# A two-block transformer layer on one core: order of bank copies in a step, chains spread over steps, a first load in six pieces, and w_o in 256 columns

## What is computed

```python
def first_block(x, mem, norm_mix, w_in, ...):
    mem_n = rmsnorm(mem, mem_norm)
    h = x
    for i in range(DEPTH):                                   # DEPTH = 1
        h = h + hybrid_mixer(rmsnorm(h, norm_mix[i]), w_in[i], ...)
        h = h + memory_cross_attention(rmsnorm(h, norm_xa[i]), mem_n, w_q[i], w_k[i], w_v[i], w_o[i])
        h = h + swiglu(rmsnorm(h, norm_ffn[i]), w_gate[i], w_up[i], w_down[i])
    return rmsnorm(h, norm_final)

def hybrid_mixer(h, w_in, ...):
    proj = h @ w_in
    z, xbc, dt_raw, sc_u, sc_b, sc_c = jnp.split(proj, IN_SPLITS, axis=-1)
...
    y_ssd = grouped_rmsnorm(y * jax.nn.silu(z), ssd_norm, SSD_GROUPS)
    v = sc_b * causal_dwconv(sc_c * sc_u, sc_conv_w)
    y_sc = grouped_rmsnorm(v, sc_norm, SC_GROUPS)
    return jnp.concatenate([y_ssd, y_sc], axis=-1) @ w_out

def second_block(x, ...):
...
        h = rmsnorm_2(x, norm_mix[i])
        p = h @ w_in[i]
        x = x + jnp.concatenate([y_a, y_b, y_c], axis=-1) @ w_out[i]   # pool, hyena and gated mixers of p
        h = rmsnorm_2(x, norm_ffn[i])
        up = dwconv3(h @ ffn_w_up[i], ffn_conv_w[i], ffn_conv_b[i])
        gate, val = jnp.split(up, 2, axis=-1)
        x = x + (jax.nn.silu(gate) * val) @ ffn_w_down[i]
    return rmsnorm_2(x, norm_final)
```

## Time and profile before

| | us |
|---|---|
| median of three executions | 2703.28 (2701.18 to 2703.99) |
| the profiled execution | 2696.7 |
| its span | 2694.9 |
| PE busy | 2639.1 |
| DVE busy | 1923.0 |
| ACT busy | 1498.2 |
| POOL busy | 391.0 |

### The profile page before, as it was taken

One profiled execution on the slowest core, in us unless ns is written; L12 is line 12 of the kernel. 1 busy time (PEld: TensorE's weight loads), 2 busy tenths in 40 slices (PEclk: granted clock), 3 DMA queues, 4 the chain that ended last, 5 costly groups with the idle time before them and its releaser, 6 DMA issues.

```text
span 2694.9 us, 38678 instructions
## 1 busy us (share of the span) xinstructions
PE 2639.1 (98%) x15034; PEld 2275.4 (84%) x15034; DVE 1923.0 (71%) x2919; ACT 1498.2 (56%) x2315; POOL 391.0 (15%) x390
## 2 busy tenths in 40 slices
PE   8999999999999999999999999999999999999998
PEld 7888888887788788888888878888888888888887
DVE  7777767868877665656565689687877677776775
ACT  6555658686555444444444456545555555555554
POOL 2111002225301010010101034011201010101012
PEclk9999999999999999999999999999999999999999
DMA  6555565565555555666666656536666666666664
GB/s 229 180 182 186 178 197 178 175 208 184 164 172 174 173 160 166 189 190 188 193 188 189 191 166 210 168 120 182 186 189 193 189 190 190 191 189 189 192 180 127
DMA packets 136559, 490.78 MB, mean 182 GB/s; under 512 B 15415, under 2 KB 16248, under 8 KB 136376
## 3 DMA queue, kind: packets, MB, share of 16 engines
q1 hardware_dynamic: 135656, 486.21, 59.6%
q10 hardware_dynamic: 720, 2.10, 0.2%
HBM read 486.12 MB, written 2.13 MB: 181 GB/s over the span
## 4 chain that ended last, share of the span: by engine, by line
PE 87%; DVE 8%; ACT 2%; issue 2%; DMA 0%; SPq 0%; DVEq 0%; ACTq 0%
PE ps L792 55%; PE ps L789 28%; DVE wl L1322 2%; ACT wh L1028 1%; DVE hT L1322 1%; DVE X L1328 1%; DVE A L1328 1%; PE ps L964 0%; PE ps L997 0%; DVE T L1328 0%; PE ps L806 0%; DVE T L1322 0%; DVE R L1322 0%; DVE Gf L1322 0%; DMA raw<-in_w_sc 0%
## 5 line engine op out<-in xcount | busy, mean ns | idle before, releaser
L1322 DVE TENSOR_TENSOR wl<-raw,wh 128x1024 fp32r<-128x1024 f32 (+1 forms) x905 | 1140.0, 1264 | 709.1 <-ACT wh L1028 708.6
L792 PE MATMUL ps<-X,wh 128*128 128x512 f32 x4848 | 1628.4, 397 | 11.9 <-DVE T L1322 5.4
L1028 ACT ACTIVATE wh<-raw 128x1024 fp32r<-128x1024 f32 (+1 forms) x905 | 953.2, 1056 | 951.6 <-PE ps L789 920.1
L789 PE MATMUL ps<-X,wl 128*128 128x256 f32 x4848 | 1225.5, 278 | 0.0
L792 PEld LDWEIGHTS ps<-X,wh 128*128 128x128 f32 x4848 | 892.6, 188 | 214.4 <-issue 10.3
L789 PEld LDWEIGHTS ps<-X,wl 128*128 128x128 f32 x4848 | 878.6, 188 | 24.0
L792 PE MATMUL ps<-XG,wh 128*128 128x512 f32 x2240 | 761.3, 399 | 21.8 <-DVE hT L1322 21.1
L789 PE MATMUL ps<-XG,wl 128*128 128x256 f32 x2240 | 571.1, 280 | 0.0
L792 PEld LDWEIGHTS ps<-XG,wh 128*128 128x128 f32 x2240 | 413.7, 189 | 118.0 <-DVE hT L1322 27.4
L789 PEld LDWEIGHTS ps<-XG,wl 128*128 128x128 f32 x2240 | 409.4, 189 | 11.4
L1792 POOL TENSOR_TENSOR hT<-hT,T 128x256 f32<-128x256 f32 x224 | 188.6, 863 | 1442.2 <-DVE hT L1322 1442.2
(11 more groups left out here) (192 smaller groups left out, 1172.0 us busy)
## 6 DMA issues: line engine op xcount, KB each, us to landing
raw<-in_w_gate SPq DMA_DIRECT2D x176, 512.0 KB, 3.8
raw<-in_w_down SPq DMA_DIRECT2D x176, 512.0 KB, 3.7
raw<-in_w_sc SPq DMA_DIRECT2D x95, 512.0 KB, 4.2
raw<-in_w_up SPq DMA_DIRECT2D x88, 512.0 KB, 3.7
raw<-in_w_val SPq DMA_DIRECT2D x88, 512.0 KB, 4.0
raw<-in_w_zx SPq DMA_DIRECT2D x80, 512.0 KB, 4.0
raw<-in_w_in SPq DMA_DIRECT2D x68, 512.0 KB, 3.7
raw<-in_w_osc SPq DMA_DIRECT2D x32, 512.0 KB, 3.7
```

What stands on the lines that cost most here:

```text
L789: t = e.matmul(bank(c, i)[:, 0:256], wl[:, b0:b0 + 128], X[:, kx * 512:kx * 512 + 256], start=False, stop=sp and kk == c.kn - 1)
L792: e.matmul(bank(c, i)[:, :], wh[:, b0:b0 + 128], X[:, kx * 512:kx * 512 + 512], start=st and kk == 0, stop=False)
L1028: return e.activation(out, in_, ACT.Copy, scale=scale)
L1322: return e.tensor_tensor(out, a, b, op)
```

## The change

It has five parts. (1) In each step the pieces `ev`, `res`, `resn` and `vcopy` are sorted to the front, ahead of the split. (2) Chains between ACT and DVE are cut into pieces of different steps: norms get `nfinb` one step behind `nfin` (with `nmm` a step later), `nfin2` gets `nfin2b`, `sn1` gets `sn1b`, `sn2` gets `sn2h` (ACT) and `sn2l` (DVE), `mgain` `mgainl`, `prod` `prodh`/`prodl`; dt5 and dt6, `zim`, `zi` and the memory's `mgain` from the fifth on move to later steps; the `evs` of the first `hv` column and of `gate` wait for the norm. (3) x comes in six loads (1, 1, 2, 4, 4, 4 tiles), of which SP issues the last three between the loads of units. (4) `w_o` uses 24 matmuls of 256 columns a unit, all into the left half, and its `resn` has two adds. (5) After steps with pieces of the scan a new matmul order, `TWOS`, is used.

```diff
         if c.kind == "rn":
-            rd += 4
+            rd += 2 if c.src == "w_o" else 4
...
-    for k, step in enumerate((0, 0, 1, 1, 2, 3, 4, 4, 5, 6, 7, 7)):
+    for k, step in enumerate((0, 0, 1, 1, 3, 3, 4, 4, 5, 6, 6, 7)):
         put(step, "xgain", 4 + k)
...
     for p in range(8):
-        put((s + 3, s + 4, s + 7, s + 8, s + 9, s + 10, s + 11, s + 12)[p], "mgain", 2 * p)
-        put(s + 3 + p + (p > 1), "nsq", (1, p))
-    put(s + 12, "nmm", 1)
-    put(s + 13, "nfin", 1)
+        d = (22, 24, 27, 28, 29, 30, 32, 33)[p]
+        put(s + d, "mgain", 2 * p)
+        put(s + d + 1, "mgainl", 2 * p)
+        put(s + 22 + p, "nsq", (1, p))
+    put(s + 31, "nmm", 1)
+    put(s + 32, "nfin", 1)
+    put(s + 33, "nfinb", 1)
...
             put(e + 1, "ev", c)
-            put(e + 1, "evs", c)
+            put(max(e + 1, U_O + 5) if c.kind == "gate" else max(e + 1, U_DOWN[0][-1].last + 6) if c.kind == "hv" else e + 1, "evs", c)
...
-                put(e + 2 + n + (n > 4), "dt%d" % n, c)
-            put(e + 8, "acsw", 0)
+                put(e + 2 + n + 3 * (n > 4), "dt%d" % n, c)
+            put(e + 9, "acsw", 0)
...
-                put(b + 9, "sn1", g)
-                s = max(b + 11, U_OSC[g // 2] + 1)
+                put(b + 10, "sn1", g)
+                put(b + 11, "sn1b", g)
+                s = max(b + 12, U_OSC[g // 2] + 1)
                 for n in range(2):
                     put(s + n, "sn2", (g, n))
+                    put(s + n + 1, "sn2h", (g, n))
+                    put(s + n + 2, "sn2l", (g, n))
...
-                    put(e + 2, "nmm2", 0)
+                    put(e + 3, "nmm2", 0)
                 if ni < 6:
-                    put(e + 2, "nmm", ni)
-                    put(e + 3, "nfin", ni)
+                    put(e + 3, "nmm", ni)
+                    put(e + 4, "nfin", ni)
+                    put(e + 5, "nfinb", ni)
...
-                    put(e + 4, "nfin2", 0)
+                    put(e + 5, "nfin2", 0)
+                    put(e + 6, "nfin2b", 0)
                     for k in range(16):
-                        put(e + 6 + k // 2, "hscale", k)
+                        put(e + 7 + k // 2, "hscale", k)
...
-                    put(b + 7 + i, "zim", 3 * hf + i)
-                    put(b + 8 + i, "zi", 3 * hf + i)
-                b += 11
+                    put(b + 8 + i, "zim", 3 * hf + i)
+                    put(b + 9 + i, "zi", 3 * hf + i)
+                b += 12
...
+    for step in at:
+        at[step].sort(key=lambda p: p[0] not in ("ev", "res", "resn", "vcopy"))
     return at
...
+TWOS = [(k, i, m) for k in range(4) for m in range(2) for i in range(2)]
+STATE = {"cbm", "ssd0", "ssd3", "sn0"}
...
-XCH = ((0, 2), (2, 4), (4, 8), (8, 12), (12, 16))
+XCH = ((0, 1), (1, 2), (2, 4), (4, 8), (8, 12), (12, 16))
...
-        for u in range(1, NRAW):
-            load(u)
-        e.dma_start(par[:, 16:NPAR], T_["par"][:, 16:NPAR]).then_inc(d_par, 16)
...
+        load(1)
+        loadx(3)
+        load(2)
+        load(3)
         for s in STEPS:
             for piece, i in PLAN[s]:
                 if piece == "split" and i + NRAW < NU:
                     load(i + NRAW)
+                    if i in (1, 2):
+                        loadx(3 + i)
...
+            elif c.src == "w_o":
...
+                    for i in range(2):
+                        b0 = (u % NW) * UN + kk * 256 + 128 * i
+                        e.matmul(bank(c, i)[:, 0:256], wh[:, b0:b0 + 128], xh, start=kk == 0, stop=False)
+                        e.matmul(bank(c, i)[:, 0:256], wh[:, b0:b0 + 128], xl, start=False, stop=False)
+                        t = e.matmul(bank(c, i)[:, 0:256], wl[:, b0:b0 + 128], xh, start=False, stop=kk == 3)
```

More of the change, by code:

```diff
@@ L230, in schedule @@
         put(step, "split", step + 3)
-    for k, step in enumerate((0, 0, 1, 1, 2, 3, 4, 4, 5, 6, 7, 7)):
+    for k, step in enumerate((0, 0, 1, 1, 3, 3, 4, 4, 5, 6, 6, 7)):
         put(step, "xgain", 4 + k)
-    for p in range(8):
[L234 to L241, removed]
-        put((s + 3, s + 4, s + 7, s + 8, s + 9, s + 10, s + 11, s + 12)[p], "mgain", 2 * p)
-        put(s + 3 + p + (p > 1), "nsq", (1, p))
-    put(s + 12, "nmm", 1)
-    put(s + 13, "nfin", 1)
-    put(s + 15, "memT", 0)
-    put(s + 16, "memc", 0)
+    for p, step in enumerate((2, 2, 3, 4, 5, 5, 6, 7)):
+        put(step, "nsq", (0, p))
+    put(8, "nmm", 0)
+    put(9, "nfin", 0)
+    put(10, "nfinb", 0)
+    s = of("z")[-1].last
+    for j in range(4):
+        put(s + 18 + 2 * j, "mload", j)
+    for p in range(8):
+        d = (22, 24, 27, 28, 29, 30, 32, 33)[p]
[5 more added lines that the diff above has]
+    put(s + 33, "nfinb", 1)
+    put(s + 35, "memT", 0)
+    put(s + 36, "memc", 0)
     for c in COLS:
@@ L346, in schedule @@
             put(e + 3, "prod", c)
+            put(e + 4, "prodh", c)
+            put(e + 5, "prodl", c)
         if c.kind == "gate" and c.i == 0:
@@ L400, in schedule @@
                 for n in range(3):
[L401 removed]
+                    put(c.first + (4, 7, 9)[n], "hout", n)
             for i in range(2):
@@ L428, in unit_orders @@
     for a, b in zip(starts, starts[1:] + [NU]):
-        order += [SIX if q == 0 else HEAD if q % 4 == 0 else EVEN for q in range(b - a)]
+        if any(piece in STATE for piece, i in PLAN.get(a - 1, ())):
+            order += [TWOS if q == 0 else HEAD if q % 4 == 1 else EVEN for q in range(b - a)]
+        else:
+            order += [SIX if q == 0 else HEAD if q % 4 == 0 else EVEN for q in range(b - a)]
     order[0] = EVEN
@@ L477, in program @@
     d_mem = [sem(f"d_mem{i}") for i in range(4)]
-    d_x = [sem(f"d_x{i}") for i in range(5)]
+    d_x = [sem(f"d_x{i}") for i in range(6)]
     d_w0 = [sem(f"d_w0_{i}") for i in range(4)]
@@ L1230, in scalar @@
                     e.activation(sacc(i), vT, ACT.Sqrt).then_inc(snA, 1)
-                if piece == "sn2":
+                if piece == "sn2h":
                     g, n = i
@@ L1255, in scalar @@
                         e.activation(Sb(i, n), Sb(i, n), ACT.Silu).then_inc(gs, 1)
-                if piece == "prod":
+                if piece == "prodh":
                     for n in range(2):
@@ L1340, in vector @@
                        ALU.subtract).then_inc(lo, 1)
-                if piece == "mgain":
+                if piece == "mgainl":
                     for k in (i, i + 1):
@@ L1363, in vector @@
                 if piece == "nfin":
-                    ps, y, u = banks[4 if i in (2, 4, 5) else 6][:, 0:256], rsb(i), tile(10 if i == 1 else 8)
+                    ps = banks[4 if i in (2, 4, 5) else 6][:, 0:256]
                     w.wait_ge(nmm, i + 1)
@@ L1476, in vector @@
                     w.wait_ge(mm, c.last + 1)
-                    for m in range(2):
+                    for m in range(1 if c.src == "w_o" else 2):
                         for n in range(2):
@@ L1574, in vector @@
                     w.wait_ge(snv, 5 * i)
-                    ts(v, banks[6][:, 0:256], 1.0 / 512, 1e-5, ALU.mult, ALU.add).then_inc(snv, 1)
+                    ts(vT, banks[6][:, 0:256], 1.0 / 512, 1e-5, ALU.mult, ALU.add).then_inc(snv, 1)
+                if piece == "sn1b":
+                    v, u, y = vT, sacc(i), srs(i)
                     w.wait_ge(snA, i + 1)
@@ L1625, in vector @@
                         tt(Sb(c, n), Sb(c, n), Sb(gate, n), ALU.mult).then_inc(pr, 1)
+                if piece == "prodl":
+                    c = i
                     for n in range(2):
```

30 lines of the change are left out of this document (22 added, 8 removed).

## The result

| | before | after |
|---|---|---|
| median, us | 2702.23 (4 runs) | 2659.56 (4 runs, 2658.39 to 2660.43) |
| profiled execution / its span | 2696.7 / 2694.9 | 2659.41 / 2657.6 |
| TensorE idle in the span | 55.8 | 27.1 |

The ratio is 0.9843, 95% interval 0.9826 to 0.9860: 42.7 us faster by the medians, 37.3 us by the two profiled executions. The forecast was 36.8 us and 2666.5 us. The kernels of the experiments ran later, beside the kernel before at medians of 2698.30, 2700.59 and 2700.21 us, so their medians are compared with 2659.56 only roughly, and what a part is worth is read from the profiles.

The account below looks back on a forecast made before the run. TensorE's work plus 55.8 us of standing still was taken as the bound, with gains only where VectorE is full. Ten terms summed to 36.8 us, so 2703.3 - 36.8 = 2666.5 us, range 2656 to 2684.

Parts of the forecast that it names:

- (a): Rival: nearly every wait goes, also at the memory norm, and the border costs nothing; gain 50 us, 2653 us; chance 0.12.
- (c): Rival, ordinary columns: sorted adds wait for TensorE's last matmul and hold up the split; slower, 2711 us; chance 0.02.
- (d): Rival: start and norms gain, but half of the banks' waits stay; time within 0.2% (5.4 us); chance 0.02.
- Rival (b): The split becomes late at the memory norm, the output projections and after zim; gain 19 us, 2684 us; chance 0.14.
- Start: First four units: the last quarter loads sooner and the half clock ends sooner; +4.3 us (3 to 5.5).
- Scan: Stretch 440 to 656 us: three waits go with the cut sn2 and the sort; +3.6 us.
- at nothing: The TWOS order, prodh/prodl and the extra issues on SP: counted as no gain, +-1 us in all.
- Memory norm: 650 to 702 us: five hT waits, about 14 us; VectorE bounds, earlier free banks help; +5 us (2.5 to 9).
- w_o: At w_o, a 2.87 us wait goes, 4.7 with extras, less 0.9 for 24 matmuls; +3.9 us (0 to 4).
- Output projections: 1500 to 1626 us: waits worth 7.7 us go as banks come free first; +7.0 us (4 to 8).
- Border: 1626 to 1680 us: old waits go, +3.1, but new waits of 3.6 and 2.0 come; -2.5 us (-5 to +2).
- zim: At zim: 3.52 us idle and a short wait, 5.5 with refill and clock; +4.9 us (2 to 6).

Follow-up runs that it names:

- the experiments on mgain, the transposes and the squares: Changed kernel with later mgain pairs: 2660.68 us; three table edits plus memT, memc three steps later: 2655.67 us; squares' sums cut to 16 columns: 2653.89 us.

## Why the prediction was right, and where not

**The frame held, and the sum was lucky.** A sum over places by TensorE's stalls gave 36.8 us for 37.3 measured between the profiles; no term has the wrong sign. But the terms miss by 0.1 to 3.1 us each, 13 us without regard to sign, and the misses cancel: the forecast is 6.7 us too low in four terms and 6.2 too high in the other six. The bounds given for the terms add up to 19.2 and 49.0 us, not to the 22 and 46 that the prediction names. Rivals (a), (c) and (d) fell. Rival (b), the split that comes late, is real at one place only, the one that the forecast had already charged.

**The basis was off by 6.6 us.** I subtracted the gain from the median, 2703.3, and got 2666.5; 2696.7 less 36.8, the profiled execution, would have been 2659.9 for 2659.56 measured. The changed kernel's profile is at its own median, the one of before was under its own. Part is the start: of four profiles with the old loads the one of before has the earliest unit 12, 1.4 us under their mean. The granted clock is another part: 37 executions of the kernel before in the later comparisons, its repeat included, run from 2694.7 to 2703.5 us, and the thirteen at a mean clock of 0.995 have a mean time of 2698.3 us, the thirteen at 0.993 one of 2700.1, the four at 0.991 or 0.992 one of 2702.6. The clocks of the three executions whose median I took are not recorded, so how the 6.6 us divide stays open.

**Start, +4.3, measured +2.1.** The load part of the mechanism is right: in all ten profiles with the new loads the first unit ends earlier (10.7 to 12.9 us) than in the four with the old ones (13.3 to 14.0). In size it is 3.1 us at unit 3 and 2.9 at unit 12 by the means of all profiles, at the lower bound of 3; the queues moved 422 GB/s in 9:11 after 416, so the rate is not what was missing. The clock part is not shown. It stands at 1.00 in 9:11 instead of 0.50, but it does so in the other three profiles with the old loads too, and in five of the ten with the new loads it is at 0.50. And +2.1 is counted from a profile of before with an early unit 12, 52.6 us; in its repeat, where the clock fell at the first norm, it is 54.3. I named the table's new steps of the squares as room and did not walk the first norm through with them. Its matmul stalls 1.45 us where it didn't before, and its second wait is 1.3 shorter. One table entry takes most of the second wait away (+1.5 at unit 12).

**Scan, +3.6, measured +6.7.** The three waits went as priced: without the new order the place still gains 3.7. The other 3.0 us are the step "at nothing", the TWOS order with the cover that a unit's length doesn't depend on it. It does: 2.77 was the length in the plain stretch, and I took it for the whole kernel. Before, 51 of the 160 units from 40 to 199 take 2.82 or 2.83 us; after, none of them.

**Memory norm, +5, measured +3.8,** inside 2.5 to 9. "VectorE bounds" is what the experiments on mgain, the transposes and the squares show, and that contended durations stay is right too. The contended row lies beside this work of GpSimd (before):

```profile
686.00 2.36 POOL L1792 TENSOR_TENSOR T<-T 128x512 f32<-128x512 f32 x2
```

The ledger missed the form of it: ScalarE waiting inside its own step for a piece that VectorE has behind a split. Of the 3.8 us, 2.7 are less waiting (10.4 to 7.7 us); the number of clock falls is two before and after.

**w_o, +3.9, measured +4.8.** The wait went. Its price of 0.9 for 24 matmuls is right (2.88 us a unit; 4.7 - 0.9 is 3.8, not 3.9), and what I left out is that fewer adds save 1.2 us of wait at the gate unit behind. That the sort alone frees the bank, I hadn't separated.

**Output projections, +7.0, measured +8.2,** and the sort alone makes 7.6. The 0.7 withheld for a full VectorE was not needed: in the same stretch VectorE is now busy 33.64 of 34 us, and no wait is left. Being full is not being late; what counts is the order in which it serves.

```profile
1563.00:1597.00 34.00, 34.00 (x198) 29.75 (x197) 33.64 (x50) 25.81 (x45) 19.56 (x14) 1.00 0.55 180
```

**Border, -2.5, measured -3.4.** The forecast new wait, 3.6 us for `wl` at unit 547, is 3.47 us at unit 547. Two errors lie under this. The chain's length was right by luck. The pieces listed add up to 16.6 us, or 17.8 with the split of unit 547, not to 17.6; measured it is 17.0 with that split. `conv` takes 1.77, not 3.6: the row I took was a later column's, beside GpSimd's work, where this column's own stood in the profile of before at

```profile
1648.17 1.66 DVE L1328 SCALAR_TENSOR_TENSOR A<-R,par,A 128x256 f32<-128x256 f32 x4
```

`evs` takes 0.76, not 1.5, and the norm's chain 3.1, not 3.6. The difference was filled by 2.2 us of idle time at hand-overs from ScalarE (0.46, 1.43 and 0.33) that I hadn't counted. And the clock fell behind this wait, here and in the six other kernels that have it, a price that I set on the old waits and forgot on the new one: unit 547 is 6.2 us longer, of which some 2.4 are the half clock (an estimate: 6.2 less the wait of 3.47 and 0.3 of refill; with the same table and wait two other kernels lose 0.9 less in this unit, at a mean clock of 0.76 instead of 0.52). The second wait of 2.0 at the next column did not come.

```profile
1621.00:1628.00 7.00, 6.10 (x19) 5.20 (x20) 6.50 (x8) 6.73 (x14) 7.00 (x6) 0.52 0.57 167
```

**zim, +4.9, measured +6.4; last feed-forward, +4.5, measured +3.4; dt, +2.0, measured +1.3.** In the first the bound of 6 was too low, by 0.4: the matmuls behind the wait at 1792 ran at the half clock and took 3.68 us, eight of them, where seven take 1.67 at the full clock, so the fall cost more than the 1.3 it was priced at. In the second two units (881 and 882) are still 0.6 us longer for `hT`. In the third the wait is gone, but units 35 and 36, behind it, are 0.3 and 0.6 us longer than before (TensorE's weight load waits 0.4 us for `wl` there), and six units behind the first norm some 0.05 each.

## What to carry to other kernels

Where one engine is stopped by banks that another must empty, put what frees a bank ahead of what is only needed later, before touching anything else: one line of sorting made half of this gain (18.5 of 37.3 us alone). A chain between two in-order engines costs each of them the other's queue; spread it over steps, but walk every engine through the new order, and set on each new wait the same prices (refill, clock) as on the old ones. If a wait that is taken away comes back under another name at the next place, the engine's total work is the bound, and the order is not what to change. Compare the sums of the waits there before calling a microsecond a gain: a fall of the clock that comes in one execution and not in the next is worth as much.

## What the runs showed of the hardware

The order of the 16 matmuls of a unit, with the same shapes and data, changed the length of some 70 units of the scan by 1 to 2% (2.77 or 2.78 us instead of 2.80 to 2.84), 3.0 us in all. Cutting GpSimd's adds from 512 columns to 16 beside VectorE's two-input operations gave 5.7 us over 16 units, with a VectorE pair at 0.87 us instead of 2.96.

The length of a wait alone did not decide whether TensorE's clock fell behind it. At unit 12 it fell in six of the eight profiles that waited 1.8 or 1.9 us there, and in one of the three that waited 3.1; at unit 229 it fell behind a wait of 3.02 us and not behind one of 3.05. A fall cost 1.5 us at both places. The first 12 units of the same kernel differed by 1.7 us between two executions, 1.6 of it by such a fall, and the 889 later ones by 0.1 in all.
